# A hybrid decoder step on one core: how the sample group's attention gets its K and V pages

## The reference

```python
past_ki = cache_idx_k[layer, page_table]          # 8 pages of 128 keys each, per sequence
score   = sum_h relu(qi . keys_ki) * wi           # 1024 past keys and the new one
_, idx  = lax.top_k(score, 256)
k_sel, v_sel = rows of cache_k / cache_v through page_table, or the new k, v
logits  = q . k_sel / 8 + t5_bias(table, q_pos - idx)
out     = softmax(logits) @ v_sel                 # 16 heads, 4 KV heads
x       = layer_norm(ALPHA * x + out @ w_out)
```

## Time and profile before

| | us |
|---|---|
| median of 3 runs | 1352.67 (1349.94 to 1353.26) |
| the profiled execution, whole | 1349.14 |
| its span in the trace | 1347.5 |
| PE busy | 1266.8 (94%) |
| DVE busy | 702.4 (52%) |
| ACT busy | 475.6 (35%) |
| POOL busy | 121.1 (9%) |
| mean granted PE clock | 0.972 of full speed |

### The profile page before, as it was taken

How to read it: one execution, slowest core, us unless ns; L and a number is a source line. 1 busy time by engine, 2 the same in 40 slices (tenths; PEclk the granted TensorE clock), 3 DMA queues, 4 the chain that set the end, 5 groups by cost and what they waited for, 6 DMA issues and landing times.

```text
span 1347.5 us, 25847 instructions
## 1 busy us (share of the span) xinstructions
PE 1266.8 (94%) x9585; PEld 1138.2 (84%) x9585; DVE 702.4 (52%) x1440; ACT 475.6 (35%) x865; POOL 121.1 (9%) x179
## 2 busy tenths in 40 slices
PE   8996988799999999999999989789999999999995
PEld 4946843455999999999999989459999999999995
DVE  2298740287576434334346763867943443433466
ACT  2341200287344223233133443863541331321332
POOL 4332543100000400000000021000000000000000
PEclk9987998799999999999999989899999999999998
DMA  6523975100221222222223413003022222222221
GB/s 192 167 82 109 287 235 170 63 1 1 79 79 64 94 86 87 94 93 93 93 82 106 125 47 100 33 1 125 33 95 94 90 84 92 93 93 94 91 81 64
DMA packets 52028, 127.86 MB, mean 95 GB/s; under 512 B 9980, under 2 KB 21156, under 8 KB 51955
## 3 DMA queue, kind: packets, MB, share of 16 engines
q1 hardware_dynamic: 38914, 105.54, 23.9%
q0 software_dynamic: 8080, 13.19, 3.6%
...
## 4 chain that ended last, share of the span: by engine, by line
PE 73%; DVE 11%; issue 8%; POOLq 3%; ACT 3%; POOL 1%; DMA 1%; ACTq 0%; SPq 0%; DVEq 0%
PE PS L528 56%; PE PS L555 6%; PE PS L745 2%; PE PS L692 2%; POOLq L347 2%; PE PS L705 2%; PE PS L719 1%; DVE YA L1486 1%; DVE PB L1620 1%; DVE PB L1645 1%; DVE YA L1473 1%; DVE X L1492 1%; DVE RSTD L1478 1%; PE PS L687 1%; DVE SC L1758 1%
## 5 line engine op out<-in xcount | busy, mean ns | idle before, releaser
L1329 DVE TENSOR_TENSOR WLO<-WRAW,WHI 128x1024 fp32r<-128x1024 f32 x118 | 145.3, 1232 | 354.2 <-ACT WHI L938 354.1
L528 PE MATMUL PS<-XH,WHI 128*128 128x260 f32 x1344 | 273.5, 285 | 1.9 <-DVE XL L1652 1.6
L938 ACT ACTIVATE WHI<-WRAW 128x1024 fp32r<-128x1024 f32 x126 | 133.5, 1059 | 401.4 <-PE PS L528 392.8
L528 PE MATMUL PS<-XH,WLO 128*128 128x260 f32 x1344 | 271.5, 284 | 0.0
L528 PE MATMUL PS<-XL,WHI 128*128 128x260 f32 x1344 | 271.2, 283 | 0.0
L528 PEld LDWEIGHTS PS<-XH,WHI 128*128 128x128 f32 x1344 | 208.1, 189 | 3.3 <-DVE XL L1652 2.3
L528 PEld LDWEIGHTS PS<-XH,WLO 128*128 128x128 f32 x1344 | 208.0, 189 | 0.0
L528 PEld LDWEIGHTS PS<-XL,WHI 128*128 128x128 f32 x1344 | 207.6, 189 | 0.0
L528 PE MATMUL PS<-HH,WHI 128*128 128x260 f32 x896 | 181.4, 284 | 0.2 <-DVE HL L1353 0.2
L528 PE MATMUL PS<-HH,WLO 128*128 128x260 f32 x896 | 180.6, 283 | 0.0
L528 PE MATMUL PS<-HL,WHI 128*128 128x260 f32 x896 | 180.2, 283 | 0.0
...
## 6 DMA issues: line engine op xcount, KB each, us to landing
...
BT<-bias_skewed SPq DMA_DIRECT2D x4, 1024.0 KB, 7.1
KVR<-cacheV POOLq DMA_DIRECT2D x20, 128.0 KB, 2.5
...
KVB<-cacheK SPq DMA_DIRECT2D x16, 128.0 KB, 2.4
KVB<-cacheK POOLq DMA_DIRECT2D x16, 128.0 KB, 2.3
```

The lines of the kernel that those rows point to most:

```text
L528: mm = pe.matmul(PS[:, 2 * slot + g, 0:TG], w[:, slot, k, :], x[:, k, TG * g:TG * g + TG], start=(k == 0 and w is WHI and x is hi), stop=( ...
L938: nc.scalar.activation(WHI[:, slot], WRAW[:, slot], ACT.Copy).then_inc(hi_done, 1)
L1329: V.tensor_tensor(WLO[:, slot], WRAW[:, slot], WHI[:, slot].bitcast(F32), ALU.subtract).then_inc(lo_dve, 1)
```

## The change

The sample attention of layer 0 is laid out anew, in five parts, all in the one diff.

- **Places.** There are 12: two more (KVX) in the space of X32 and one (KVW) in that of WRAW. All eight K sets have a place of their own and are loaded while units 0 to 9 run; V sets 8, 9, 10 and 15 don't wait for any K to be used. X32 is loaded a second time, after the last V set (`x_back`, waited for by DVE at unit 14), and units 16 and 17 are loaded after the last V set too.
- **Column tiles.** The sequences go in two groups of four. The four of a group write four different sets of 32 output rows, with a 32-column query tile, and their matmuls stand next to one another: for K in the order c0, then sequence; for V in the order page, then sequence, with the new token's product first. V's results lie at rows 0, 32, 64 and 96.
- **Three queues for V.** Of each V set SP loads 4 or 5 pages, POOL 2, ACT 1 or 2 (`KV_SPLIT`); the order of sets is `V_ORDER`. `load_values` reads the page numbers of four sets into registers, then waits, then issues. POOL no longer loads pages between the low parts. ACT also issues the BT loads, now in four DMAs of 128 columns of all heads, and a step of the prompt attention waits for its own one.
- **Early digits.** Digit 0 comes after 16 prompt rounds in place of 22, and every digit one slot later (digit 0 in the middle of unit 6). Units 12 and 13 are in the static loop, in which ACT makes the next high part before it evacuates a unit.
- **The samples' output inside the prompt attention.** The turn of V's result, and its split, stand in `sample_a` after the first two logits steps.

```diff
-KV_PLACE = (0, 1, 2, 3, 7, 8, 4, 5, 6, 7, 8, 4, 5, 3, 6, 7)
+K_ORDER = (0, 2, 4, 6, 1, 3, 5, 7)
+KV_PLACE = (9, 10, 7, 8, 0, 1, 2, 3, 4, 5, 6, 9, 10, 7, 8, 11)
+KV_SPLIT = ((8, 8), (8, 8), (8, 8), (0, 8), (8, 8), (8, 8), (0, 8), (0, 8),
+            (4, 6), (4, 6), (4, 6), (5, 7), (5, 7), (5, 7), (5, 7), (4, 6))
+V_ORDER = (8, 9, 10, 15, 11, 12, 13, 14)
-SLOT_OF = (0, 1, 2, 3, 4, 5, 6, 7, 9, 10, 11)
-SP_FROM = (0, 0, 8, 8, 8, 6) + 10 * (5,)
+SLOT_OF = (1, 2, 3, 4, 5, 6, 7, 8, 10, 11, 12)
-STATIC_UNITS = 12
+STATIC_UNITS = 14
+def kv_pages(n):
+    a, b = KV_SPLIT[n]
+    return (0, a), (a, b), (b, NPG)
-    return max([m + 1 for m in range(n) if KV_PLACE[m] == KV_PLACE[n]], default=0)
+    return max([m // 4 * 4 + 4 for m in range(n) if KV_PLACE[m] == KV_PLACE[n]], default=0)
+        KVX = place("KVX", [P, 2, NPG, 256], at=14 * TOK)
...
+        KVW = place("KVW", [P, NPG, 256], at=words[0])
...
+        def page_number(eng, n, pg):
+            b = K_ORDER[n] if n < DB else n - DB
+            return eng.value_load(PT[0:1, bass.ds(pg + b * NPG, 1)],
+                                  min_val=0, max_val=POOL_PAGES - 1)
+        def fetch_page(eng, n, pg, page):
...
             eng.dma_start(dst.rearrange("p o n -> p (o n)"),
                           cache[bass.ds(page, 1), :, :].rearrange("o p n -> (o p) n")
-                          ).then_inc((kv_sp if eng is nc.sync else kv_pool)[pl], 16)
...
+        def load_values(eng, q):
+            for group in (V_ORDER[:4], V_ORDER[4:]):
+                pages = {n: [page_number(eng, n, pg) for pg in range(*kv_pages(n)[q])]
+                         for n in group}
                 eng.wait_ge(unit_done, A_OUT)
-            if kv_before(n):
-                eng.wait_ge(kv_used, kv_before(n))
+                for n in group:
+                    if n == 15:
+                        eng.wait_ge(lo_pool, LO_SKIP)
+                    if kv_before(n):
+                        eng.wait_ge(kv_used, kv_before(n))
+                    for pg, page in zip(range(*kv_pages(n)[q]), pages[n]):
+                        fetch_page(eng, n, pg, page)
...
+            sp.wait_ge(nat_mm, 5)
+            sp.wait_ge(x_hi, 1)
+            sp.wait_ge(x_lo, 1)
             with sp.Fori(1, POOL_LO[0] // 2 + 1) as i:
                 for s in range(2):
                     sp.wait_ge(lo_dve, i * 2 + (s - 1))
                     load_unit(i * 2 + s, s)
-                for b in range(2):
-                    for q in range(2):
-                        load_page(sp, b, i * 2 + (q - 2))
-            with sp.Fori(POOL_LO[0] // 2 + 1, POOL_LO[1] // 2 + 1) as i:
+                    for n in ((4, 5), (0, 1))[s]:
+                        for q in range(2):
+                            load_page(sp, n, i * 2 + (q - 2))
+            sp.wait_ge(ds_mm, 3)
+            with sp.Fori(0, NPG) as pg:
+                load_page(sp, 2, pg)
+            with sp.Fori(POOL_LO[0] // 2 + 1, POOL_LO[1] // 2) as i:
                 for s in range(2):
                     sp.wait_ge(lo_pool, i * 2 + (s - 1 - POOL_LO[0]))
                     load_unit(i * 2 + s, s)
-            sp.wait_ge(ds_sum, 1)
-            for n in range(5, 2 * DB):
-                wait_place(sp, n)
-                with sp.Fori(SP_FROM[n], NPG) as pg:
-                    load_page(sp, n, pg)
-                if n == DB + 1:
-                    sp.wait_ge(toe_skew, 16 * 4)
-                    for pl in range(3):
-                        sp.wait_ge(kv_used, pl + 1)
-                        load_bias(pl)
-            sp.wait_ge(kv_used, KV_PLACE.index(3, 4) + 1)
-            load_bias(3)
+            load_values(sp, 0)
+            sp.wait_ge(kv_used, 2 * DB)
+            for s in range(2):
+                load_unit(POOL_LO[1] + s, s)
+            sp.dma_start(X32[:], io["xT"]).then_inc(x_back, 16)
...
-            for n in (2, 3):
+            for n in (6, 7):
                 with pool.Fori(0, NPG) as pg:
                     load_page(pool, n, pg)
             pool.wait_ge(ds_mm, 3)
             nc.gpsimd.memset(QB[:], 0.0).then_inc(z_qb, 1)
-            wait_place(pool, 4)
-            with pool.Fori(0, 4) as pg:
-                load_page(pool, 4, pg)
-            for u in range(POOL_LO[0], POOL_LO[0] + 2):
+            with pool.Fori(0, NPG) as pg:
+                load_page(pool, 3, pg)
+            for u in range(*POOL_LO):
                 low_part(u, u % 2)
-                for q in range(2):
-                    load_page(pool, 4, 4 + 2 * (u % 2) + q)
-            with pool.Fori(POOL_LO[0] // 2 + 1, POOL_LO[1] // 2) as i:
-                for s in range(2):
-                    low_part(i * 2 + s, s)
-                    load_page(pool, 5, i * 2 + (s - POOL_LO[0] - 2))
-            for n in range(6, 2 * DB):
-                wait_place(pool, n)
-                with pool.Fori(0, SP_FROM[n]) as pg:
-                    load_page(pool, n, pg)
-                if n == DB - 1:
-                    pool.wait_ge(nat_ev, 5)
-                    for b in range(DB):
-                        pool.dma_start(VNEW[0:1, b, :], NAT[b:b + 1, 4, HD + IDXH:NATW]
-                                       ).then_inc(vnew_in, 16)
+            pool.wait_ge(nat_ev, 5)
+            pool.wait_ge(unit_done, A_OUT)
+            for b in range(DB):
+                pool.dma_start(VNEW[0:1, b, :], NAT[b:b + 1, 4, HD + IDXH:NATW]
+                               ).then_inc(vnew_in, 16)
+            load_values(pool, 1)
...
-            for b in range(DB):
-                wait_kv(b)
+            for quad in (range(0, 4), range(4, 8)):
+                for n in quad:
+                    wait_kv(n)
                 for gp in range(2):
-                    end = b == DB - 1 and gp == 1
-                    q = QB[:, (2 * b + gp) * P:(2 * b + gp + 1) * P]
-                    for half in range(2):
-                        mm = pe.matmul(PSF[:, 512 * half:512 * half + 512], q,
-                                       kv_place(b)[:, 4 * half:4 * half + 4, gp * P:(gp + 1) * P],
-                                       start=False, stop=end)
-                    last = pe.matmul(PSF[:, 1024:1025], q, UQ[:, 4 + gp, SEQ + b:SEQ + b + 1],
-                                     start=False, stop=end)
-                mm.then_inc(kv_used, 1)
-            last.then_inc(dl_mm, 1)
+                    end = quad[0] == 4 and gp == 1
+                    for c0 in (0, 512, 1024):
+                        for n in quad:
+                            b = K_ORDER[n]
+                            r = slice(32 * (b // 2), 32 * (b // 2) + 32)
+                            q = QB[:, (2 * b + gp) * P + r.start:(2 * b + gp) * P + r.stop]
+                            if c0 < 1024:
+                                mm = pe.matmul(PSF[r, c0:c0 + 512], q,
+                                               kv_place(n)[:, c0 // P:c0 // P + 4,
+                                                           gp * P:(gp + 1) * P],
+                                               start=False, stop=end)
+                                if gp == 1 and c0 == 512:
+                                    mm.then_inc(kv_used, 1)
+                            else:
+                                mm = pe.matmul(PSF[r, 1024:1025], q,
+                                               UQ[:, 4 + gp, SEQ + b:SEQ + b + 1],
+                                               start=False, stop=end)
+            mm.then_inc(dl_mm, 1)
...
+            def sample_out(b):
+                return PS[32 * (b % 4):32 * (b % 4) + NH, 4 + b // 4, 0:256]
             for b in range(DB):
-                n = DB + b
-                wait_kv(n)
-                o = PSF[0:NH, 2048 + 256 * b:2048 + 256 * b + 256]
-                rows = slice(NH * b, NH * b + NH)
+                pe.matmul(sample_out(b), PNEW[0:1, NH * b:NH * b + NH], VNEW[0:1, b, :],
+                          start=True, stop=False)
+            for quad in (range(0, 4), range(4, 8)):
+                for b in quad:
+                    wait_kv(DB + b)
                 for k in range(NPG):
-                    mm = pe.matmul(o, PTD[:, k, rows], kv_place(n)[:, k, :], start=(k == 0),
-                                   stop=False)
-                mm.then_inc(kv_used, 1)
-                pe.matmul(o, PNEW[0:1, rows], VNEW[0:1, b, :], start=False, stop=True
-                          ).then_inc(ov_mm, 1)
-            for b in range(DB):
-                pe.wait_ge(ov_ev, b // 2 + 1)
-                for gp in range(2):
-                    c = (2 * b + gp) * NH
-                    mm = pe.transpose(PS[:, 0, c:c + NH], OV[:, b, gp * P:(gp + 1) * P],
-                                      CST[0:NH, 0:NH])
-            mm.then_inc(do_mm, 1)
-            pe.wait_ge(do_lo, 1)
+                    for b in quad:
+                        mm = pe.matmul(sample_out(b), PTD[:, k, NH * b:NH * b + NH],
+                                       kv_place(DB + b)[:, k, :], start=False,
```

(42 more changed lines are left out.)

122 lines of the change are left out of this document (59 added, 63 removed).

## The result

The changed kernel takes 1300.49 us (median, 1299.31 to 1303.05), the kernel before 1351.38 beside it: ratio 0.9625, interval 0.9604 to 0.9646. The forecast was 1289, range 1274 to 1306, with 1284 to 1294 for the likeliest case. So the direction and the size of the gain were right (50.9 us of some 63), the time lies in the range, and it lies above the likeliest case, 11.5 us over the forecast. That the miss is not larger is in part luck: the trace puts unit 14 14.8 us later than forecast (294.47 for 279.7), but the forecast had added 3.5 us for the distance between the profiled execution and the median, and here the two are the same (1300.45 and 1300.49).

What follows compares the result with a forecast made beforehand. GpSimd's queue, issuing one V page per 1.50 us, was taken to set V's end. V ending 65.1 us earlier, less 1.9 after it, gives 63.2: 1349.14 becomes 1286, plus 3.5 to the median, 1289; range 1274 to 1306.

Steps and rivals of the forecast that it cites:

- Part 1: Early digits, up to unit 13: digit 0 at 104.3, PE idles less, unit 13 ends at 151.3, 12.0 us earlier.
- Parts 2 and 3: Sample attention: K pages loaded ahead cost 0; four column tiles side by side take 9 us for K, 4.7 per four V sequences.
- Rival (b): Column tiles don't run four at once: 1297 with two (0.27 shared with two other rivals), 1325 with none (0.06).
- Part 4: Between K's end and the values: ACT's page reads and issues delay its exponential; cost 1.6 us, between 0 and 6.
- Part 5: V pages on three queues: SP's last issue at 179.1, landing 5 us later, V ends at 188.7, 65.1 us earlier.
- Rival (c): V page-number reads ahead of the waits are paid after unit 13: 8 us, 1297; 0.27 shared with two other rivals.
- rival (a): DMA engines become the bound for V and BT: V ends at 195 to 197, 1297; 0.27 shared with two others.
- Part 6: Samples' output inside prompt attention: 2.9 us go away, first normalise waits 4.8 for the split; net +1.9.
- Rival (d): V pages come sooner: V ends at 178, where DVE's rounds take over, 1279 us; chance 0.16.
- (e): Slower than before: BT quarters in 512-byte runs land late for the prompt attention's first steps, up to 1412; chance 0.03.

Runs made afterwards that it cites:

- e7: e3 with the early digits undone: 22 prompt rounds ahead of digit 0, every digit one slot earlier, two rounds behind the last; 1308.54 us.
- e8: e3 with ACT loading no V pages; GpSimd takes its twelve (28 in all), SP keeps 36; 1300.22 us.
- e5: e3 without reads ahead: every queue reads a V page's number right before issuing that page, after the waits; 1301.69 us.
- e2: Changed kernel with GpSimd's subtraction for the low weights of units 8 to 15 cut to 32 of 1024 columns; 1294.91 us.
- e9: e3 with V page numbers read early, spread: six behind each SP load of units 10 to 15, some on GpSimd and ACT; 1285.42 us.
- e3: Changed kernel with GpSimd's subtraction for the low weights done in eight instructions of 128 columns, nothing left out; 1297.47 us.
- e11: e9 with BT loads on SP behind V, and the samples' output split moved behind the first step's exponentials and first normalise; 1279.11 us.

## Why the prediction was right, and where it was off

The path that it named is the one that the runs show: digits, then reads and issues, then the last pages. e7, e8 and e5 each undo a piece of it, and V's end moves by 12.4, 5.7 and 6.6 us. Off were a collision that it didn't see and the price of the reads.

**Part 1** held: 12.0 forecast, 11.9 by e7, and unit 13's end within 0.6 us in e2. What failed is a step that it didn't have: the digits' new times brought VectorE's steps onto GpSimd's subtractions, 4.7 us by e2 of the 5.3 by which unit 13 was late. Rows of both engines stood in the trace of before, and laying the new times of the one beside the other would have shown it.

**Parts 2 and 3** held. K was not waited for and took 9.3 (forecast 9.0). That this is so near is partly luck: eight instructions of 512 columns took 1.7 us in the first two groups, at a granted clock of 0.50 (the lower level, after PE had idled 4.35 us), and about 0.9 in the last four at 1.00, where the forecast had 1.0 throughout. Four sequences of V took 4.9 (4.7). Rival (b) is out: sixteen instructions in 1.89.

**Part 4** was priced at 1.6. In the changed kernel ACT's exponential started 1.0 us behind the maximum (176.32, with its table load at 175.03 behind ACT's last issue; the maximum ended at 175.31). In e9, where ACT's issues were over at 167.4, it started at once (170.15, maximum to 170.11). So the mechanism was there, at 1.0, and did not decide, since the first values waited 5.67 for pages.

**Part 5** is the part that was off, in its size. Issues of 0.54 were right for the first block (8.7 for 8.6). "The 16 reads happen before unit 13 ends" was wrong: I let SP be done with unit 15 at 143.6; it was 149.35, 146.0 without the collisions (e3). And a read was 0.42, from 0.27 of the load and 0.15 of register work; it takes 0.57 to 0.66 on SP and about 0.7 on ACT; the queue stands between its rows. The Trainium skill (DMA: Bandwidth & Descriptors, Latency and other measured facts) puts the floor of a tensor load at about 600 ns; SP's 0.57 to 0.66 lies there, the 0.27 of the profile's row does not. Rival (c) so came true in part (2.9 us, 4.0 in e3), and rival (a) in part: issues of the second block at 0.67 in place of 0.54, and 7.0 to landing. That e9 ends V at 189.5, near the forecast's 188.7, is no support for these terms, as said there.

**Part 6**: forecast +1.9 from V's end to unit 14, measured +0.6; its named cost is shown by e11.

Rival (d) did not come, and (e) is out: a BT quarter took 16.2 us in 512-byte runs, 2.3 times as long as before, but the first softmax waited for PE's logits, not for it.
